# Modulation products on VectorE beside the first projection, TensorE only summing over partitions

## The reference

```
mod_ctx = silu(c_ctx) @ w_ada + b_ada          # w_ada: 1024 x 6144
mod_lat = silu(c)     @ w_ada + b_ada
shift1, scale1, gate1, shift2, scale2, gate2 = split(mod, 6)
h = rms_norm(x, g0) * (1 + scale1) + shift1
z = h @ w_in                                   # columns: u_f, u_p, q, k, v, o, gates, merge
y = parallel_mixer(z) ;  x = x + gate1 * rms_norm(y, g1)
h = rms_norm(x, g2) * (1 + scale2) + shift2
x = x + gate2 * rms_norm((silu(a) * b) @ w_ffn_out, g3)    # a, b = split(h @ w_ffn_in)
```

## Time and profile before

| what | value |
|---|---|
| median of 3 runs | 1754.23 us (1751.44 to 1754.8) |
| the profiled execution | 1757.72 us |
| its span | 1755.6 us |
| mean granted TensorE clock | 0.993 |
| busy in the span: PE, DVE, ACT, POOL | 1706.8, 910.3, 630.5, 222.2 us |

### The profile page before, as it was taken

How to read it: one execution, slowest core, us unless ns; L and a number is a source line. 1 busy time by engine, 2 the same in 40 slices (tenths; PEclk the granted TensorE clock), 3 DMA queues, 4 the chain that set the end, 5 groups by cost and what they waited for, 6 DMA issues and landing times. The chain is left out here.

```text
span 1755.6 us, 24577 instructions
## 1 busy us (share of the span) xinstructions
PE 1706.8 (97%) x9622; PEld 1596.7 (91%) x9622; DVE 910.3 (52%) x1544; ACT 630.5 (36%) x1108; POOL 222.2 (13%) x340
## 2 busy tenths in 40 slices
PE   7999999999999999999999899999999999999996
PEld 3899999989999999998988799999999999888885
DVE  5400002343434444456878984555555553679885
ACT  6312113242222222233656582222222222454542
POOL 1400001322222233311000000000000001000000
PEclk9999999999999999999999999999999999999998
DMA  9544445764455556679777322222222214668683
GB/s 350 227 174 148 161 155 194 237 213 143 148 173 184 176 190 210 195 242 273 247 227 227 132 79 72 75 76 76 71 76 73 70 66 153 183 182 247 180 281 125
DMA packets 155290, 294.68 MB, mean 168 GB/s; under 512 B 12730, under 2 KB 91901, under 8 KB 155179
## 3 DMA queue, kind: packets, MB, share of 16 engines
q1 hardware_dynamic: 111312, 161.64, 28.4%
q0 software_dynamic: 27536, 91.31, 15.7%
q10 hardware_dynamic: 16336, 40.29, 6.5%
HBM read 225.42 MB, written 67.82 MB: 167 GB/s over the span
## 5 line engine op out<-in xcount | busy, mean ns | idle before, releaser
L668 PE MATMUL bank<-h_hi,w_hi 128*128 128x384 f32 x1080 | 372.3, 345 | 3.7 <-DVE h_lo L2615 3.1
L670 PE MATMUL bank<-h_hi,w_lo 128*128 128x384 f32 x1080 | 362.4, 336 | 0.0
L669 PE MATMUL bank<-h_lo,w_hi 128*128 128x384 f32 x1080 | 362.0, 335 | 0.0
L1955 DVE TENSOR_TENSOR w_lo<-raw,w_hi 128x1024 fp32r<-128x1024 f32 x152 | 185.3, 1221 | 238.2 <-ACT w_hi L1463 238.0
L668 PEld LDWEIGHTS bank<-h_hi,w_hi 128*128 128x128 f32 x1080 | 203.4, 188 | 21.3 <-ACT z_st L1523 10.1
L1463 ACT CAST w_hi<-raw 128x1024 fp32r<-128x1024 f32 x152 | 157.5, 1052 | 161.5 <-DMA raw<-in_w_stream 121.1
L669 PEld LDWEIGHTS bank<-h_lo,w_hi 128*128 128x128 f32 x1080 | 203.6, 189 | 0.1
L670 PEld LDWEIGHTS bank<-h_hi,w_lo 128*128 128x128 f32 x1080 | 203.2, 188 | 0.0
L670 PE MATMUL bank<-w_hi,a_lo 128*128 128x512 f32 x352 | 136.9, 389 | 0.0
L669 PE MATMUL bank<-w_lo,a_hi 128*128 128x512 f32 x352 | 136.9, 389 | 0.0
L668 PE MATMUL bank<-w_hi,a_hi 128*128 128x512 f32 x352 | 136.9, 389 | 0.0
(11 more groups left out here) (354 smaller groups left out, 3282.0 us busy)
## 6 DMA issues: line engine op xcount, KB each, us to landing
raw<-in_w_stream SPq DMA_DIRECT2D x142, 512.0 KB, 4.6
z_scratch<-z_st ACTq DMA_DIRECT2D x44, 576.0 KB, 3.1
raw<-in_w_stream SPq DMA_DIRECT2D x90, 256.0 KB, 4.3
raw<-in_w_ada SPq DMA_DIRECT2D x35, 512.0 KB, 5.6
mg<-z_scratch ACTq DMA_DIRECT2D x24, 576.0 KB, 6.3
a_raw<-f_scratch SPq DMA_DIRECT2D x44, 256.0 KB, 3.4
a_raw<-f_scratch SPq DMA_DIRECT2D x22, 320.0 KB, 3.7
zt<-z_scratch POOLq DMA_DIRECT2D x27, 256.0 KB, 4.3
```

Of the source, the lines that this page charges most:

```text
L668: pe.matmul(out, a_hi, b_hi, start=start, stop=False)
L669: pe.matmul(out, a_hi, b_lo, start=False, stop=False)
L670: return pe.matmul(out, a_lo, b_hi, start=False, stop=stop)
L1955: dve.tensor_tensor(w_lo[:, slot], raw[:, slot], w_hi[:, slot].bitcast(F32), ALU.subtract).then_inc(s_wlo, 1)
```

## The change

The two matmuls of each modulation unit of this stage leave PE. DVE multiplies the slot by the scalar column of `c_pad` and adds into `ada_acc`, one 128x512 accumulator for each vector and for each of two blocks in turn (`ada_pair`): 8 operations for each `zi`, each waiting for the last but one. `ada_acc` is laid into the first two tiles of `x_in`, so the first operation waits until all nine stores of `x_in` have landed. PE then sums `ada_acc` over the partitions (`ada_sum`), by 8 matmuls for a block, with a 128x128 part of `ada_acc` stationary and one column of ones moving, straight into the columns of bank 4. It stands after the second column block of the next even `zi` (the turn stood after the first). ACT's copy `ada_out` goes. Blocks 0 to 3 and the last turn of the start stay as they were.

`s_arow` now counts DVE's operations, and SP waits for it before the loads that replace a modulation unit: the load of projection unit `zi` waits for `ada_done(zi - 2, 1)`, all 8 operations of `zi` - 2. PE counts `s_unit` up by three at the end of each projection unit. On DVE the split of unit `zi` + 1 stands ahead of the operations of `zi`.

```diff
--- before.py
+++ after.py
@@ -278,6 +278,7 @@
         xr = sb(s2, "xr", [P, 3, D])
         c_pad = sb(s2, "c_pad", [P, KT, ADA_M])
         ada_row = sb(s2, "ada_row", [P, 2, ADA_W])
+        ada_acc = x_in[:, 0:2].rearrange("p b (v n) -> p b v n", v=2)
         rows = sb(s2, "rows", [V_ROWS, P])
         s2.close()
 
@@ -691,6 +692,10 @@
 
             return ADA_ORDER[blk] if isinstance(blk, int) and blk < len(ADA_ORDER) else blk
 
+        def ada_done(zi, v):
+
+            return zi * 8 + (ADA_FIRST // ADA_G + 4 * (v + 1))
+
         def h_order(g, k):
 
             return k // KH * (KH * NG) + KH * g + k % KH
@@ -782,7 +787,10 @@
                 for u in range(RAW):
                     n0 = ADA_FIRST + 3 * u
                     if not (first and u == 0):
-                        sp.wait_ge(s_unit, i * 12 + (n0 - RAW + 1))
+                        if first and u == 1:
+                            sp.wait_ge(s_unit, n0 - RAW + 1)
+                        else:
+                            sp.wait_ge(s_arow, i * 32 + ada_done(u - 2, 1))
                         load(n0 % RAW, w_stream[bass.ds(i * RAW + u, 1)])
                     if first and u == 0:
                         sp.wait_ge(s_unit, n0 + 1 - RAW + 1)
@@ -790,7 +798,10 @@
                         sp.wait_ge(s_whi, i * RAW + u)
                         sp.wait_ge(s_wlo, i * RAW + u)
                     load((n0 + 1) % RAW, w_ada[bass.ds(i * (2 * RAW) + (ADA_FIRST + 2 * u), 1)])
-                    sp.wait_ge(s_unit, i * 12 + (n0 + 2 - RAW + 1))
+                    if first and u == 0:
+                        sp.wait_ge(s_unit, n0 + 2 - RAW + 1)
+                    else:
+                        sp.wait_ge(s_arow, i * 32 + ada_done(u - 1, 0))
                     load((n0 + 2) % RAW, w_ada[bass.ds(i * (2 * RAW) + (ADA_FIRST + 2 * u + 1), 1)])
 
             z1_turn(0, True)
@@ -802,8 +813,10 @@
                 if n == U_G + 1:
                     sp.wait_ge(s_whi, Z1_UNITS)
                     sp.wait_ge(s_wlo, Z1_UNITS)
+                elif n == U_G:
+                    sp.wait_ge(s_arow, ada_done(Z1_UNITS - 2, 1))
                 else:
-                    sp.wait_ge(s_unit, n - RAW + 1)
+                    sp.wait_ge(s_arow, ada_done(Z1_UNITS - 1, n - U_G - 2))
                 load(n % RAW, w_stream[n - SHIFT_A:n - SHIFT_A + 1])
             for n in range(U_G + RAW, U_F):
                 unit(n, n % RAW, w_stream[n - SHIFT_A:n - SHIFT_A + 1])
@@ -925,6 +938,15 @@
                                   K["sum2"], start=True, stop=True)
                 m.then_inc(s_aturn, 1)
 
+            def ada_sum(blk, b):
+
+                pe.wait_ge(s_arow, (blk - ADA_FIRST // ADA_G) * 16 + (ADA_FIRST // ADA_G + 16))
+                for q in range(ADA_W // P):
+                    for v in range(2):
+                        m = pe.matmul(bank[4][:, bass.ds(blk * (2 * ADA_W // P) + (2 * q + v), 1)],
+                                      ada_acc[:, b, v, ktile(q)], ones[:, 0:1], start=True, stop=True)
+                m.then_inc(s_aturn, 1)
+
             def spread_row(c):
 
                 if c == 0:
@@ -990,7 +1012,7 @@
                     wh, wl = W(z_number(zi0, shift) % SPL, k)
                     r = slice(b * GW, (b + 1) * GW)
                     m = mm3(pe, bank[b][:, 0:GW], wh, wl, h_hi[:, k, r], h_lo[:, k, r], k == 0, k == KT - 1)
-                m.then_inc(s_unit if b == NG - 1 else s_zmm, 1)
+                m.then_inc(s_unit if b == NG - 1 else s_zmm, 3 if b == NG - 1 and shift is None else 1)
 
             def first_unit():
 
@@ -1003,7 +1025,7 @@
                             r = slice(b * GW, (b + 1) * GW)
                             m = mm3(pe, bank[b][:, 0:GW], wh, wl, h_hi[:, k, r], h_lo[:, k, r], k == 0, k == KT - 1)
                         if half:
-                            m.then_inc(s_unit if b == NG - 1 else s_zmm, 1)
+                            m.then_inc(s_unit if b == NG - 1 else s_zmm, 3 if b == NG - 1 else 1)
                         elif b == 0:
                             ada_turn(ADA_FIRST // ADA_G - 1, 1)
 
@@ -1014,11 +1036,8 @@
                     first_unit()
                 for b in range(0 if not (first and zi0 == 0) else NG, NG):
                     z_part(zi, zi0, None, b, first)
-                    if b == 0 and zi0 % 2 == 0 and not (first and zi0 == 0):
-                        ada_turn(i * 2 + (blk - 1), (blk - 1) % 2)
-                for v in range(2):
-                    n0 = ADA_FIRST + 3 * zi0 + 1 + v
-                    ada_unit(zi * 3 + (ADA_FIRST + 1 + v), n0, zi0 % 2 * 2 + v, blk % 2, i * 2 + (blk - 1))
+                    if b == 1 and zi0 % 2 == 0 and not (first and zi0 == 0):
+                        ada_sum(i * 2 + (blk - 1), (blk - 1) % 2)
 
             def project():
                 for u in range(4):
@@ -1028,8 +1047,8 @@
                         z_unit(i * 4 + u, u, False, i)
                 for b in range(NG):
                     z_part(ZI_G, ZI_G, SHIFT_A, b)
-                    if b == 0:
-                        ada_turn(ADA_UNITS // ADA_G - 1, 1)
+                    if b == 1:
+                        ada_sum(ADA_UNITS // ADA_G - 1, 1)
 
             def t_tile(c):
 
@@ -1537,8 +1556,6 @@
             def project():
                 for zi in range(Z1_UNITS):
                     z_unit(zi, zi, None, DH ** -0.5 if 8 <= zi < 12 else 1.0)
-                    if zi % 2:
-                        ada_out(ADA_FIRST // ADA_G + zi // 2, z_number(zi, None) + 2)
                 for n in range(U_G + 1, U_G + AHEAD + 1):
                     split(n, n)
                 for b in range(NG):
@@ -1989,13 +2006,41 @@
                 dve.tensor_copy(eps[:], eps[:]).then_inc(s_mod, 1)
                 dve.wait_ge(s_mod, 2)
 
+            def ada_pair(i, u):
+
+                blk, b = ADA_FIRST // ADA_G + u // 2, u // 2 % 2
+                if u == 0:
+                    dve.wait_ge(s_xps, 16 * NT)
+                if u % 2 == 0:
+                    dve.wait_ge(s_aturn, i * 2 + (blk - 1))
+                for w in range(2):
+                    n0 = ADA_FIRST + 3 * u + 1 + w
+                    slot = n0 % RAW
+                    dve.wait_ge(s_raw[slot], i * (3 * 16) + slot_count(n0, n0))
+                    for kk in range(2):
+                        k = u % 2 * 4 + w * 2 + kk
+                        for v in range(2):
+                            src, scale = raw[:, slot, kk * ADA_W:(kk + 1) * ADA_W], c_pad[:, k, v:v + 1]
+                            if k:
+                                dve.wait_ge(s_arow, i * 32 + (ada_done(u, w) - 5 + 2 * kk + v))
+                                x = dve.scalar_tensor_tensor(ada_acc[:, b, v], src, scale, ada_acc[:, b, v], ALU.mult, ALU.add)
+                            else:
+                                x = dve.tensor_scalar(ada_acc[:, b, v], src, scale, None, ALU.mult)
+                            x.then_inc(s_arow, 1)
+
             def project():
+                dve.wait_ge(s_cpad, 1)
                 with dve.Fori(0, Z1_UNITS // 4 - 1) as i:
                     for u in range(4):
                         split(i * 12 + (ADA_FIRST + 3 * u + AHEAD), ADA_FIRST + 3 * u + AHEAD, i * 4 + (u + 1))
-                for u in range(Z1_UNITS - 4, Z1_UNITS - 1):
-                    split(ADA_FIRST + 3 * u + AHEAD, ADA_FIRST + 3 * u + AHEAD, u + 1)
-                for n in range(U_G, U_G + AHEAD + 1):
+                        ada_pair(i, u)
+                for u in range(Z1_UNITS - 4, Z1_UNITS):
+                    if u < Z1_UNITS - 1:
+                        split(ADA_FIRST + 3 * u + AHEAD, ADA_FIRST + 3 * u + AHEAD, u + 1)
+                    else:
+                        split(U_G, U_G)
+                    ada_pair(0, u)
+                for n in range(U_G + 1, U_G + AHEAD + 1):
                     split(n, n)
                 modulation_rest()
```

## The result

The kernel with the change takes 1758.55 us at the median of 14 runs (1753.73 to 1761.49), the kernel before 1754.34 in 14 runs beside them (1751.32 to 1755.83). The ratio is 1.0021, interval 1.0014 to 1.0029: slower by 0.2%, 4 us. The forecast was 1759.4, slower. The profiled execution has a span of 1758.0 us against 1755.6.

What follows compares the result with a forecast made beforehand. TensorE alone was taken to bound the first projection. Unit 2's later start +11.9, clock +2.4, removed pairs -16.8 and sums +7.7 gave +5.2 us; against a median of 1754.23 the forecast was 1759.4, range 1754.5 to 1769.

Steps and rivals of the forecast that it cites:

- Stores complete at 75.7: Before unit 2: all nine stores of `x_in` land at 75.7 us (74.9 to 80.1), letting the first VectorE product start.
- Products of unit 0, 4.9 us: On VectorE after the stores land: unit 0's eight operations take 4.9 us before unit 2's load may go.
- Load 4.6: Unit 2's weight load, after unit 0's products: 4.6 us to land, the median of such loads (3.5 to 6.2).
- Clock 2.4: TensorE after its gap before unit 2: half rate for 3 to 6 us costs 2.4 us (1.6 to 3.1).
- Removed, 16.8: TensorE from unit 2 on: 14 pairs of modulation units leave, at 1.20 us each, saving 16.8 us.
- sums, 7.7: TensorE in this stage: eight turns become eight partition sums, adding 7.7 us (7.2 to 11.0).
- Sum: Whole change: later unit 2 start +11.9, clock +2.4, removed pairs -16.8, partition sums +7.7, together +5.2 us.
- B: Rival for the whole kernel: the delay at its short bounds, or cheaper partition sums; +0 to +3.5 us, chance 0.16.
- C, faster: Rival at unit 2: stores land before the products are wanted, unit 2 isn't held; 11.5 us gained, 1742.7, chance 0.08.
- D, the slots bound the stage: Rival over the stage: VectorE's chain and load outlast TensorE, loop 14.7 us against 13.4; +13 more, 1772, chance 0.08.

Runs made afterwards that it cites:

- second trace: Profile of the unaltered change, timed once more: 1758.23 us against 1755.1 for the kernel before, ratio 1.0022.

## Why the prediction was right

The mechanism and the sign were right, and the time was 0.9 us off, which is in part luck: the terms below add up to 2 us less than forecast, and the same kernel timed again gave +3.1 and not +4.2. The mechanism is shown, not only argued, by the undone wait (-12.5 us) and by the wait put alone into the kernel before (+8.0). Step by step:

- *Stores complete at 75.7.* In the second trace, whose stores are issued at the times of before's, the last of them is issued at 64.8 and lands at most 11.1 us later, by 75.9, and the first product starts at 76.12; 75.8 was forecast. The argument that the missing loads leave their share of the queues to the stores held.
- *Products of unit 0, 4.9 us.* 4.86 (75.11 to 79.97), from starts 0.66 and 0.40 apart, as sized by slope from two other shapes.
- *Load 4.6.* It took 3.7. The median over the span is of loads that share the queues; this one met no store, only the modulation load issued 0.42 us behind it. Unit 2 is 11.1 us late in place of 11.9.
- *Clock 2.4.* 1.6 and, in the second trace, 1.85: at the lower end of the bounds 1.6 and 3.1.
- *Removed, 16.8; sums, 7.7.* The sums cost 8 x 0.89 = 7.1. The pairs' 1.20 us are borne out by unit 2 to gate unit: 198.15 - 14 x 1.20 + 7 x 0.89 + 1.6 = 189.2, measured 188.82.
- *Sum.* 11.1 + 1.6 - 16.8 + 7.1 = +3.0; the stage shows +2.6 to +2.8, the medians +4.2 and +3.1. So the working of +5.2 was 2 us too high, in three terms of which each was taken a little dear: landing, clock, sums. The 1.2 us between the +3.0 of the trace and the +4.2 of the medians are within the interval and have no cause shown. By the ratio's interval the time is +2.5 to +5.1 us, so *B* (up to +3.5) isn't excluded as a size.
- *C, faster.* Its size was right, and it is what the kernel gives when the wait and the stores are away: 11.5 forecast, 12.7 measured. It didn't happen because the stores took until 74.9 us in the first trace and 75.9 in the second, not 70.5.
- *D, the slots bound the stage.* Refuted for this change: the loop is 11.4 us, not 12.4, against 13.4 of TensorE. The median landing of the ring's loads fell from 5.5 to 3.9 us, as its counter-argument said. The loop does decide once it is longer, which the experiment with more work on VectorE showed: at 14.2 us a loop 15.5 us were lost, some 10 of them outside the one gap ahead of unit 4.

Of the experiments four were off in size. The wait for two stores gave -1.3 us in place of -3 to -4: unit 2's start and the half rate were both taken too cheap. The extra work on VectorE gave 15.5 in place of 20 to 28: the loop's load was taken as 4.6 us and is 3.7. The wait in the kernel before gave 8.0 in place of 10 to 11.5, and half the sums 4.6 in place of 7; there the traces show 9.5 and 7.1, and only the medians are smaller.

The warning of idle gaps in the Trainium skill (TensorE: Matmul & The Clock Gate, "Why this matters for your kernels") agrees with the clock at 0.50 after the gap of 12.64 us, which cost 1.6 us beside the gap itself. The Trainium skill's figure of 358 GB/s (SBUF — State Buffer, "A bandwidth-pool intuition that's wrong") is no ceiling in the trace of after either, where the queues of this one core moved 410 GB/s in the stretch from 73 to 74 us.

## What to carry to other kernels

Before work is moved to an idle engine, ask where its output lies and who still reads that place: an accumulator laid into a tile that a DMA is storing makes the first write wait for the store, and every load that waits for that write stands behind it. Moving the work was worth 12.7 us (1755.02 against 1742.3), and the change as it stood lost 16 against that (1758.55 against 1742.3). The place of its output cost 12.5 of them, which another idle tile gave back; the other 3.7 were the price of nine stores leaving at once, which stores that leave one by one gave back. A store that nobody waits for can still be dear as the neighbour of a load that somebody does.

## What the runs showed of the hardware

- After a gap, the time at half rate did not follow the gap's length: gaps of 3.04, 7.41, 7.50, 12.64 and 12.63 us were followed by some 3.0, 5.7, 4.3, 3.2 and 3.7 busy us at a granted clock of 0.50. In the kernel with more work on VectorE, after a gap of 3.89 us, the clock stayed at 1.00 for the first 1.3 busy us, and only then came 3.4 us at 0.50. What sets it is open.
- A load of 512 KB took 3.7 us from its issue to the cast with no store in flight, and 7.6 to 8.7 among stores of 512 KB in another queue.
- Eight passes with a 128x128 fp32 stationary tile and one moving column took 0.89 us of TensorE's time, as much as eight with two columns in the turns of before (0.90 us). So the moving columns don't set the price; that the weight loads do (eight in 1.03 us in the earlier trace rows) is argued, not shown.
- `scalar_tensor_tensor` of 128x512 in fp32 with a scalar per partition took 746 ns and let the next start after 0.66 us; `tensor_scalar` took 480 and 0.40.
